# Three of eight pairs of k-tiles of the FFN input products as seven block products instead of eight, in a transformer block on one core

## The reference, cut to what matters

```python
def swiglu(x, w_in, w_out):                  # x 256x2048, w_in 2048x11264, w_out 5632x2048
    gate, up = jnp.split(x @ w_in, 2, axis=-1)
    return (jax.nn.silu(gate) * up) @ w_out
h = x + 0.5 * swiglu(rmsnorm(x, g1), w_in1, w_out1)
...
h = h + 0.5 * swiglu(rmsnorm(h, g2), w_in2, w_out2)
out = rmsnorm(h, g_final)
```

## Time and profile before

| | |
|---|---|
| median of 3 runs | 2148.08 us (2147.76 to 2148.32) |
| span of the profiled execution, first to last instruction | 2145.7 us |
| PE busy | 2137.6 us, 100% |
| DVE busy | 1192.2 us, 56% |
| ACT busy | 1010.0 us, 47% |
| DMA queue of SP | 67.2% of 16 engines |
| mean granted clock of TensorE | 0.999 |

### The profile page before, as it was taken

How to read it: one execution, slowest core, us unless ns; L and a number is a source line. 1 busy time by engine, 2 the same in 40 slices (tenths; PEclk the granted TensorE clock), 3 DMA queues, 4 the chain that set the end, 5 groups by cost and what they waited for, 6 DMA issues and landing times.

```text
span 2145.7 us, 26770 instructions
## 1 busy us (share of the span) xinstructions
PE 2137.6 (100%) x9585; PEld 1774.9 (83%) x9585; DVE 1192.2 (56%) x1187; ACT 1010.0 (47%) x1157; POOL 39.0 (2%) x50
## 2 busy tenths in 40 slices
PE   9999999999999999999999999999999999999998
PEld 8888888888888888888888888888888888888887
DVE  6555555555555576566555656665555555554444
ACT  6444444443444465456544555554444444444343
POOL 0000000000000031000000000000000000000000
PEclk9999999999999999999999999999999999999999
DMA  8766677666666677765587766676676666765554
GB/s 317 240 217 213 212 226 220 213 210 194 226 218 212 217 266 240 237 213 185 177 285 239 234 207 186 201 241 216 211 230 214 212 211 225 223 212 191 194 187 157
DMA packets 183139, 468.15 MB, mean 218 GB/s; under 512 B 16928, under 2 KB 67488, under 8 KB 182944
## 3 DMA queue, kind: packets, MB, share of 16 engines
q1 hardware_dynamic: 180912, 459.91, 67.2%
q0 software_dynamic: 1728, 6.82, 0.9%
q10 hardware_dynamic: 432, 0.53, 0.1%
HBM read 439.41 MB, written 27.79 MB: 218 GB/s over the span
## 4 chain that ended last, share of the span: by engine, by line
PE 99%; issue 0%; DMA 0%; DVE 0%; ACT 0%; POOLq 0%; DVEq 0%; POOL 0%
PE acc L1640 32%; PE acc L1642 32%; PE acc L1643 32%; PE acc L1754 1%; PE aux L1937 0%; PE aux L1910 0%; PE aux L1906 0%; PE aux L1933 0%; PE aux L1932 0%; PE aux L1905 0%; PE aux L1847 0%; DMA arrived<-in_first_cols 0%; PE acc L1719 0%; PE acc L1717 0%; PE acc L1715 0%
## 5 line engine op out<-in xcount | busy, mean ns | idle before, releaser
L1052 DVE TENSOR_TENSOR w_lo<-raw,w_hi 128x1024 fp32r<-128x1024 f32 x765 | 935.9, 1227 | 884.1 <-ACT w_hi L629 882.8
L629 ACT ACTIVATE w_hi<-raw 128x1024 fp32r<-128x1024 f32 x765 | 808.1, 1060 | 1043.1 <-PE acc L1643 1014.4
L1640 PE MATMUL acc<-w_hi,a_hi 128*128 128x512 f32 x1384 | 539.0, 389 | 0.0
L1642 PE MATMUL acc<-w_lo,a_hi 128*128 128x512 f32 x1384 | 538.5, 389 | 0.0
L1643 PE MATMUL acc<-w_hi,a_lo 128*128 128x512 f32 x1384 | 538.5, 389 | 0.0
L1640 PE MATMUL acc<-w_hi,b_hi 128*128 128x512 f32 x1216 | 474.5, 390 | 0.0
L1642 PE MATMUL acc<-w_lo,b_hi 128*128 128x512 f32 x1216 | 473.2, 389 | 0.0
L1643 PE MATMUL acc<-w_hi,b_lo 128*128 128x512 f32 x1216 | 473.2, 389 | 0.0
L1640 PEld LDWEIGHTS acc<-w_hi,a_hi 128*128 128x128 f32 x1384 | 259.8, 188 | 54.7 <-issue 0.9
L1643 PEld LDWEIGHTS acc<-w_hi,a_lo 128*128 128x128 f32 x1384 | 259.8, 188 | 54.1
L1642 PEld LDWEIGHTS acc<-w_lo,a_hi 128*128 128x128 f32 x1384 | 259.8, 188 | 53.5
(11 more groups left out here) (195 smaller groups left out, 687.6 us busy)
## 6 DMA issues: line engine op xcount, KB each, us to landing
raw<-in_ffn_w_in SPq DMA_DIRECT2D x349, 512.0 KB, 4.2
raw<-in_ffn_w_out SPq DMA_DIRECT2D x176, 512.0 KB, 4.2
raw<-in_w_mix_in SPq DMA_DIRECT2D x80, 512.0 KB, 4.6
raw<-in_w_ckv SPq DMA_DIRECT2D x64, 512.0 KB, 4.4
memq<-bounce SPq DMA_DIRECT2D x196, 128.0 KB, 3.8
bounce<-stage SPq DMA_DIRECT2D x37, 512.0 KB, 5.0
raw<-in_w_mix_out SPq DMA_DIRECT2D x32, 512.0 KB, 4.7
raw<-in_w_cq SPq DMA_DIRECT2D x32, 512.0 KB, 4.3
```

The costliest lines, as they stand in the source:

```text
L629: eng.activation(w_hi[:, u % RING], raw[:, u % RING], ACT.Copy).then_inc(w_hi_done, 1)
L1052: eng.tensor_tensor(w_lo[:, u % RING], raw[:, u % RING], w_hi[:, u % RING].bitcast(f32), ALU.subtract).then_inc(w_lo_done, 1)
L1640: eng.matmul(dst, x_hi[:, rows], w_hi[:, slot, i], start=start and i == 0, stop=False)
L1642: eng.matmul(dst, x_hi[:, rows], w_lo[:, slot, i], start=False, stop=False)
```

## The change

In the ten looped passes of each FFN input stage, k-tiles 2s and 2s+1 for s = 0, 1, 2 are handled for gate and up together, as a 2x2 block product: activations in four blocks (2 token halves x 2 k-tiles), weights in four blocks b11, b12 (first k-tile, gate and up columns), b21, b22 (second k-tile). Strassen's scheme gives the four result blocks from seven block products instead of eight. The other five units of gate and five of up stay as they are.

- A pass still has 16 units through the ring (`PAIR_ORDER`): fast 0 (two units), gate 3, gate 4, fast 1 (two units), gate 5, gate 6, fast 2 (two units), gate 7, up 3, up 4 to up 7. The units at places 0, 4 and 8 hold b12 and b11, those at 1, 5 and 9 hold b21 and b22.
- Per fast pair DVE makes three sums of weight blocks in four additions of 512 columns (`weight_sums`, which begins when both units have been loaded; one addition is done in place in `raw`), ACT makes their hi part (1536 columns, `t_hi_part`) and DVE their lo part (`t_lo_part`). The fast units themselves are split as before.
- The sums of activation blocks (`mix_hi`, `mix_lo`) are made once per stage, in the first pair of chunks (`mix_parts`, at places 9, 11, 13).
- PE does 21 matmuls for the two units of a fast pair. Four of the seven sums collect in `tp` and `aux`, which the stage did not use or used for `turn`; `turn` now writes to `stage`.
- At the end of a pass the results are put together: ACT copies one sum, DVE does four additions of 512 columns and two subtractions of 1024 (the second, `up_drained`, in the next pass). PE starts the next pass after `gate_read`, and does the first product into the up banks after `up_read`.
- SP sends `stage` ahead of the load at place 7 and fetches it ahead of the load at place 8.
- The new tiles lie over `h` and `row_gain`, so `h` is loaded again in `ffn_out`, ahead of the loads at its places 4 to 7, and POOL's loads of `row_gain` come after the last fast pair.
- The weights are laid out in the new order on the host, before the kernel.

```diff
+FAST = 3
+def pair_order():
+    plain = [(0, u) for u in range(FAST, U8)] + [(1, u) for u in range(FAST, U8)]
+    order = []
+    for s in range(FAST):
+        order += [("fast", s), ("fast", s)] + plain[:2]
+        plain = plain[2:]
+    return order + plain
...
+GATE_END = PAIR_ORDER.index((0, U8 - 1)) + 1
+UP_START = PAIR_ORDER.index((1, FAST))
+SEND_AT = 7
...
+        sum_p1 = tp[:].rearrange("p (b a) n -> p b (a n)", b=2)[:, 0]
+        sum_p5 = tp[:].rearrange("p (b a) n -> p b (a n)", b=2)[:, 1]
+        sum_p6, sum_p7 = aux[:, 0], aux[:, 1]
+        stage4 = stage[:].rearrange("p t (a n) -> p (t a) n", a=2)
+        copy_p1 = junk
...
+                    for p in range(PAIR):
+                        if p == SEND_AT:
+                            send(number(TURNS, hid) - 1 + j, stage[:], hid_done, silus[base] + j)
+                        if p == SEND_AT + 1:
+                            fetch(number(TURNS, hid) - 1 + j, first=base == FFN1_IN)
+                        load(w, PAIR * j + p, base + PAIR * j, p)
...
+                    if u == RING:
+                        eng.wait_ge(w_used, fast_done(in_base))
+                    if RING <= u < RING + DC:
+                        h_again(in_base, u - RING)
...
+                def fast_hi(j, s):
+                    p = FAST_AT[s]
+                    eng.wait_ge(t1_done, fast_count(base, j, s) + 1)
+                    split(base, j, p, PAIR)
+                    eng.wait_ge(t_summed, fast_count(base, j, s) + 1)
+                    if s:
+                        eng.wait_ge(t_used, fast_count(base, j, s))
+                    eng.activation(t_hi_part[:], t_raw[:], ACT.Copy).then_inc(t_hi_done, 1)
+                    split(base, j, p + 1, PAIR)
+                def pair(j, hid_dst):
+                    for s in range(FAST):
+                        fast_hi(j, s)
+                        split(base, j, FAST_AT[s] + 2, PAIR)
+                        if s == FAST - 1:
+                            fill_hi(turned, number(TURNS, hid) + j, hid_dst, src=stage4)
+                        split(base, j, FAST_AT[s] + 3, PAIR)
+                    for p in range(4 * FAST, PAIR - 3):
+                        split(base, j, p, PAIR)
+                    eng.wait_ge(w_used, base + PAIR * j + FAST_END)
+                    eng.activation(copy_p1, sum_p1, ACT.Copy).then_inc(p1_copied, 1)
+                    split(base, j, PAIR - 3, PAIR)
+                    split(base, j, PAIR - 2, PAIR)
+                    eng.wait_ge(gate_added, fast_pairs[base] + j)
+                    for t in range(NT):
+                        last = eng.activation(stage[:, t], stage[:, t], ACT.Silu,
+                                              scale=rstd[:, stat(rs), t:t + 1])
+                    last.then_inc(silu_done, 1)
+                    split(base, j, PAIR - 1, PAIR)
...
+                def up_drained(j):
+                    eng.wait_ge(gate_read, silus[base] + 1 + j)
+                    eng.wait_ge(w_used, base + PAIR + PAIR * j)
+                    eng.tensor_tensor(shared[:], acc[:, NT:2 * NT], shared[:], ALU.subtract).then_inc(up_read, 1)
...
+                def weight_sums(j, s):
+                    p = FAST_AT[s]
+                    r = p % RING
+                    count = fast_count(base, j, s) + 1
+                    b12, b11, b21, b22 = raw[:, r, 0], raw[:, r, 1], raw[:, r + 1, 0], raw[:, r + 1, 1]
+                    eng.wait_ge(w_loaded[r], loads_of(base, j, p))
+                    eng.wait_ge(w_loaded[r + 1], loads_of(base, j, p + 1))
+                    eng.tensor_tensor(t_raw[:, 0], b12, b22, ALU.add)
+                    eng.tensor_tensor(b12, b12, b11, ALU.add).then_inc(t1_done, 1)
+                    eng.wait_ge(t1_done, count)
+                    eng.tensor_tensor(t_raw[:, 1], b12, b22, ALU.add).then_inc(t2_done, 1)
+                    eng.wait_ge(t2_done, count)
+                    eng.tensor_tensor(t_raw[:, 2], t_raw[:, 1], b21, ALU.add).then_inc(t_summed, 1)
+                def unit_lo(j, p):
+                    split(p, base + PAIR * j + p)
+                def fast_lo(j, s):
+                    weight_sums(j, s)
+                    unit_lo(j, FAST_AT[s])
+                    eng.wait_ge(t_hi_done, fast_count(base, j, s) + 1)
+                    eng.tensor_tensor(t_lo_part[:], t_raw[:], t_hi_part[:].bitcast(f32), ALU.subtract
+                                      ).then_inc(t_lo_done, 1)
+                    unit_lo(j, FAST_AT[s] + 1)
+                def pair(j, hi, lo):
+                    done = fast_pairs[base] + j
+                    for s in range(FAST):
+                        fast_lo(j, s)
+                        if s == FAST - 1:
+                            turn(number(TURNS, hid) - 1 + j, stage4)
+                        unit_lo(j, FAST_AT[s] + 2)
+                        if s == 0:
+                            up_drained(j - 1)
+                        if s == FAST - 1:
+                            fill_lo(split_number(hid) - 1 + j, lo, hi, src=stage4)
+                        unit_lo(j, FAST_AT[s] + 3)
+                        if s == 0:
                             hidden(j - 1)
+                    for p in range(4 * FAST, PAIR - 3):
+                        unit_lo(j, p)
+                    eng.wait_ge(p1_copied, done)
+                    eng.tensor_tensor(shared[:, 0], sum_p6, copy_p1, ALU.add).then_inc(p6_added, 1)
+                    unit_lo(j, PAIR - 3)
+                    eng.wait_ge(p6_added, done)
+                    eng.tensor_tensor(shared[:, 1], shared[:, 0], sum_p7, ALU.subtract).then_inc(p7_added, 1)
+                    eng.wait_ge(w_used, base + PAIR * j + GATE_END)
+                    eng.tensor_tensor(stage[:, 0], acc[:, 0], copy_p1, ALU.add)
+                    eng.wait_ge(p7_added, done)
+                    eng.tensor_tensor(stage[:, 1], acc[:, 1], shared[:, 1], ALU.add).then_inc(gate_added, 1)
+                    unit_lo(j, PAIR - 2)
+                    eng.wait_ge(gate_added, done)
+                    p5 = sum_p5.rearrange("p (a n) -> p a n", a=1).broadcast_to([P, NT, CH])
+                    eng.tensor_tensor(shared[:], shared[:], p5, ALU.subtract).then_inc(gate_read, 1)
+                    unit_lo(j, PAIR - 1)
...
+                def three(dst, x, w, start, stop):
+                    eng.matmul(dst, x[0], w[0], start=start, stop=False)
+                    eng.matmul(dst, x[0], w[1], start=False, stop=False)
+                    return eng.matmul(dst, x[1], w[0], start=False, stop=stop)
+                def block_of(k, t):
+                    rows = slice(t * P, (t + 1) * P)
+                    return hi[:, k, rows], lo[:, k, rows]
+                def ring_block(p, i):
+                    return w_hi[:, p % RING, i], w_lo[:, p % RING, i]
+                def sum_block(i):
+                    return t_hi_part[:, i], t_lo_part[:, i]
+                def fast(j, s):
+                    p = FAST_AT[s]
+                    unit = base + PAIR * j + p
+                    start, stop = s == 0, s == FAST - 1
+                    s3, s1, s2 = [(mix_hi[s][:, i], mix_lo[s][:, i]) for i in range(3)]
+                    eng.wait_ge(w_lo_done, unit + 1)
+                    three(sum_p1, block_of(UK * s, 0), ring_block(p, 1), start, stop)
+                    three(sum_p5, s1, ring_block(p, 0), start, stop).then_inc(w_used, 1)
+                    eng.wait_ge(t_lo_done, fast_count(base, j, s) + 1)
+                    three(sum_p7, s3, sum_block(0), start, stop)
+                    three(sum_p6, s2, sum_block(1), start, stop)
+                    three(acc[:, 1], block_of(UK * s + 1, 1), sum_block(2), start, False).then_inc(t_used, 1)
+                    eng.wait_ge(w_lo_done, unit + 2)
+                    three(acc[:, 0], block_of(UK * s + 1, 0), ring_block(p + 1, 0), start, False)
+                    if s == 0:
+                        eng.wait_ge(up_read, silus[base] + j)
+                    three(acc[:, NT], block_of(UK * s, 1), ring_block(p + 1, 1), start, False).then_inc(w_used, 1)
+                def plain(j, p):
+                    side, u = PAIR_ORDER[p]
+                    eng.wait_ge(w_lo_done, base + PAIR * j + p + 1)
+                    for i in range(UK):
+                        for t in range(NT):
+                            start = p == UP_START and i == 0 and t == 1
+                            stop = u == U8 - 1 and i == UK - 1
+                            last = three(acc[:, NT * side + t], block_of(UK * u + i, t), ring_block(p, i), start, stop)
```

More of the change, by code:

```diff
@@ L26 @@
 OUT_SCALE = float(D) ** -0.5
+PAIR = 2 * U8
+FAST = 3
[6 more added lines that the diff above has]
+    return order + plain
+PAIR_ORDER = pair_order()
+FAST_AT = [PAIR_ORDER.index(("fast", s)) for s in range(FAST)]
+FAST_END = FAST_AT[-1] + 2
+GATE_END = PAIR_ORDER.index((0, U8 - 1)) + 1
+UP_START = PAIR_ORDER.index((1, FAST))
+SEND_AT = 7
+MIX_AT = [9, 11, 13][:FAST]
 FFN1_IN = 0
@@ L346, in encoder_block @@
```

(40 more changed lines are left out.)

160 lines of the change are left out of this document (98 added, 62 removed).

## The result

The changed kernel takes 2176.5 us (2174.8 to 2178.5) against 2148.2 us of the kernel before: 1.0132 times as long, with an interval of 1.0117 to 1.0146. It is slower, as forecast, by 28 us where 42 were predicted.

What follows compares the result with a forecast made beforehand. VectorE was to bound the changed kernel: 39.3 + 1.5 + 0.2 + 4.3 + 0.3 = 45.6 us a pass against 43.52, +42 us over twenty passes, span 2188, time 2190 us. Range 2130 to 2220; the forecast alone 2153 to 2220.

Steps and rivals of the forecast that it cites:

- DVE is the bound of a pass: Looped FFN passes: VectorE's work of 39.3 us plus waits makes 45.6 us, longer than TensorE's 41.49.
- The overlap of 0.09 us: VectorE's queue: an instruction that awaits nothing starts 0.09 us before the one ahead of it ends.
- read as no overlap: Rival for VectorE's new sequences: no overlap, +3.1 us a pass, 2253 us; chance 0.07 together with a fallen clock.
- 0.5 us for ACT's hi part: Each fast pair: VectorE waits 0.5 us for ScalarE's hi part of the weight sums, three times a pass, 1.5 us.
- no wait for the load of place 5: Sums of the second fast pair: 0.3 us of wait at a landing of 4.7, 0 at 4.2, 1.9 at 6.3.
- the wait for the load of place 9: Before the third fast pair's sums: VectorE waits 4.3 us a pass, between 2.2 and 5.2.
- both paths issue it at the same time, right behind a fetch: Load of place 9: slot freed by split 5 and SP's queue behind the fetch coincide; landing taken as 6.3 us.
- The lower bound of 4.2 us: Landing of the load of place 9 in the best case, 4.2 us, giving a wait of 2.2 us.
- `mix_parts` costs nothing: First pair of chunks: some 3 us of VectorE three times, covered by 1.49 us idle per unit; otherwise 9 us a stage.
- PE stays the bound: Rival for the passes: VectorE's waits vanish and TensorE sets their length, 2107 us; to 2143 us, chance 0.20.
- Loads as when alone: Rival for the load waits: landing after 4.2 us, a pass of 43.2 us, 2142 to 2152 us; chance 0.11.
- PE's clock falls: Rival: a TensorE pause of 2 to 3 us each pass lowers its clock, 2238 us; chance 0.07 together with no overlap.

Runs made afterwards that it cites:

- Both doublings: The changed kernel with one VectorE split done twice in each pass: at place 13, 2198.0 us; in another run at place 7, 2173.9 us.
- the fetch at 10: The changed kernel with the fetch ahead of the load of place 10 instead of 8: 2160.1 us.
- the late `mix`: The changed kernel with ScalarE's and VectorE's parts of the activation sums made later in the first pair of chunks: 2167.6 us; also combined with other edits.
- `turn` late: The changed kernel with weight sums' lo part one unit later, activation sums later, fetch at place 12, transpose behind the split of place 11: 2119.7 us.
- the order alone: The changed kernel with both fast units split before ScalarE's hi part and VectorE's lo part of the weight sums: 2137.0 us.
- order, fetch at 12: The changed kernel with both fast units split before the sums' hi and lo parts, and the fetch ahead of the load of place 12: 2142.6 us.
- order, fetch at 10: The changed kernel with both fast units split before the sums' hi and lo parts, and the fetch ahead of the load of place 10: 2141.7 us.

## Why the prediction was right and where it was off

**Right: DVE is the bound of a pass, and the load of place 9 its longest wait.** Both doublings and the fetch show it. The durations held: the lo part of 1536 columns lasts 1.76 us (1.68 + 0.09 was taken), ACT's hi part 1.48. The additions start 0.61, 0.72 and 0.73 us apart (0.59, 0.715, 0.715). The overlap of 0.09 us held in the new sequences too, all of it on this timeline of DVE in one pass of the changed kernel:

```profile
246.93 1.76 DVE L1322 TENSOR_TENSOR t_lo_part<-t_raw,t_hi_part 128x1536 fp32r<-128x1536 f32 x1 [0.42 <-ACT t_hi_part L822]
248.61 3.49 DVE L1185 TENSOR_TENSOR w_lo<-raw,w_hi 128x1024 fp32r<-128x1024 f32 x3
254.97 0.69 DVE L1306 TENSOR_TENSOR t_raw<-raw 128x512 f32<-128x512 f32 x1 [2.88 <-DMA raw<-in_ffn_w_in]
255.58 0.68 DVE L1307 TENSOR_TENSOR raw<-raw 128x512 f32<-128x512 f32 x1
256.30 0.69 DVE L1309 TENSOR_TENSOR t_raw<-raw 128x512 f32<-128x512 f32 x1
257.03 0.69 DVE L1311 TENSOR_TENSOR t_raw<-t_raw,raw 128x512 f32<-128x512 f32 x1
```

246.93 + 1.76 is 0.08 us after the next split started. By the rule of the Trainium skill (VectorE: DVE Perf Modes, Terms), read as no overlap, the sum would have been 2253; the trace disagrees.

**Right: 0.5 us for ACT's hi part** (0.42 measured, three times), and no wait for the load of place 5.

**Mis-sized: the wait for the load of place 9**, 2.64 us against 4.3, and with it nearly the whole error of a pass (44.2 against 45.6). The step that failed is "both paths issue it at the same time, right behind a fetch", with a landing of 6.3 us. DVE's path to the end of split 5 was right, the other was too long. SP's queue in that pass, start and time to the end of issue, then the load's landing and the send's:

```profile
242.89 0.41 SPq L455 DMA_DIRECT2D bounce<-stage  x1
...
245.98 1.97 SPq L464 DMA_DIRECT2D memq<-bounce  x4
248.16 11.20 SPq L448 DMA_DIRECT2D raw<-in_ffn_w_in  x5
...
L448 SPq DMA_DIRECT2D raw<-in_ffn_w_in x1: 352/352/352, 250.0 to 250.0; - x1
...
DMA to landing us min/median/max: 4.9/4.9/4.9
...
L455 SPq DMA_DIRECT2D bounce<-stage x1: 406/406/406, 242.9 to 242.9; - x1
...
DMA to landing us min/median/max: 3.1/3.1/3.1
```

The send landed after 3.1 us, not 4.2, so the fetch was out by 247.9, two us before the load of place 9 at 250.0. That load had only the load of place 8 close ahead, by 1.8 us; the fetch's pieces, with 2.3 to 2.5 us each, had landed. It took 4.9 us, and 4.3 to 5.0 in five passes. A send of on-chip data to a buffer had been priced like a load of weights, and the 6.3 us of three loads 1.1 us apart was too high a price for these neighbours. That is 1.4 us a pass, 28 us in all. The lower bound of 4.2 us was none either: with the fetch at 10 this load lands after 3.8. In the other direction, 0.27 us of a wait for ACT's hi part of what `turn` made was not listed.

**Wrong: `mix_parts` costs nothing, "under the 1.49 us that DVE idles in each unit".** The idle time was there, but it was itself the time in which DVE waits for ACT. The sums that ACT waits for can't be made in it: they stand in DVE's queue behind a split that needs ACT. So cover was read in one engine where the chain goes through two. The prediction named a price of 9 us a stage if the cover were gone. The whole loss outside the loops is 12.0 us for both stages, and the late `mix` takes 6 to 7 of it away. The remaining 5 us, and the longer first passes, were not told apart. The timeline shows at FFN1's entry ACT's table load of 1.28 us behind a wait of 1.35 on `a_lo`, then DVE's 1.30 on silu before its first sums, and PE's 2.56 before the first matmul of the loop; no run took these away.

**The rivals.** *PE stays the bound* did not hold in this order, but it names what another order reaches. *Loads as when alone* gave 2142 to 2152; the landing of 4.9 us lies between 4.2 and 6.3, and passes of 44.2 alone would be 2148 + 14 = 2162, still 10 us above it. *PE's clock falls* once a pass, as the rule of HAM oscillation (the Trainium skill, TensorE: Matmul & The Clock Gate) would have it: in passes it didn't, through the pauses of PE in each (columns of the earlier trace rows):

```profile
212.00:214.00 2.00, 1.92 (x9) 1.27 (x7) 1.97 (x3) 1.73 (x2) 0.00 (x0) 1.00 0.26 107
214.00:216.00 2.00, 1.51 (x6) 1.05 (x6) 1.58 (x2) 2.00 (x3) 0.00 (x0) 1.00 0.21 35
```

This doesn't refute the rival as it stands. It supposed one pause of 2 to 3 us a pass. On PE's timeline of this pass no matmul starts more than 0.7 us late, and the longest idle time in any pass is 1.4 us. Where PE did pause for longer, at the entries, the clock fell (the last section).

So the total came out near the forecast partly by luck, by two errors that offset each other: some 25 us too many in the loops (20 x 45.6 = 912 against 887.3), 12 too few outside them.

## What to carry to other kernels

A scheme that trades matmuls for additions on another engine is decided by the order in that engine's queue. The busy sum was 39.7 us of 41.5 and fitted; what decided were two hand-overs between engines and the distance in time from the instruction that frees a slot to the one that needs its next load. Idle time of an engine is cover for new work only if what it waits for doesn't wait for that new work. And a DMA moved out of a queue's way can cost again where it then runs: beside loads that the same edits have brought close together, or ahead of a reader that now waits for it.

## What the runs showed of the hardware

**PE's clock at the entries.** In the passes of the changed kernel PE pauses, for up to 1.4 us, and stays at 2.4 GHz; at the entries of its loops it doesn't. In the fastest kernel (`turn` late) PE waits 3.94 us for the first lo part of FFN1's loop, as the timeline of PE shows:

```profile
54.82 0.79 PE L1889 MATMUL tp<-w_hi,a_hi 128*128 128x512 f32 x1 [3.94 <-DVE w_lo L1185]
55.41 0.63 PE L1890 MATMUL tp<-w_lo,a_hi 128*128 128x512 f32 x1
55.84 0.63 PE L1891 MATMUL tp<-w_hi,a_lo 128*128 128x512 f32 x1
```

The granted clock of the same kernel around it, in stretches of 2 us, is then 0.50, the level of 1.2 GHz, and matmuls start 0.43 us apart instead of 0.227:

```profile
52.00:54.00 2.00, 0.00 (x0) 0.00 (x0) 1.93 (x4) 1.61 (x2) 0.00 (x0) 0.80 0.00 0
54.00:56.00 2.00, 1.18 (x3) 0.99 (x4) 2.00 (x3) 2.00 (x3) 0.00 (x0) 0.50 0.18 27
...
58.00:60.00 2.00, 2.00 (x6) 1.52 (x6) 2.00 (x3) 0.00 (x0) 0.00 (x0) 0.50 0.70 252
60.00:62.00 2.00, 2.00 (x10) 1.65 (x9) 2.00 (x3) 0.00 (x0) 0.00 (x0) 1.00 0.86 229
```

The twelve matmuls from 54.82 to 60.20 take 5.4 us, where 12 x 0.2267 is 2.7. So the pause of 3.9 us costs up to 6.6. The changed kernel shows the same at the entry of FFN1's loop, after a pause of 2.56 us, and at that of FFN2's, after 1.86 us (0.50 from 1486 to 1488). At FFN1's:

```profile
60.00:62.00 2.00, 1.93 (x5) 1.35 (x5) 2.00 (x3) 1.37 (x2) 0.00 (x0) 0.50 0.51 197
```

The length of the pause alone doesn't decide. In the changed kernel PE also waits 2.50 us before 42.95, in the first pair of chunks, and the granted clock stays at 1.00. With the order alone, where the same code makes the same pause of 2.49 us before 42.34, it falls to 0.50. All four pauses of 3.9 us in the kernels with the late `mix` and three pairs were followed by a fall, pauses of 1.0 to 1.5 us (between 20 and 2100 us of the spans) by none. Nothing here shows what decides in between. One such fall more or less, some 1 to 3 us, can be part of why executions of one kernel differ; no trace of a second execution shows it.

**Loads beside a fetch and beside each other.** The landing of one load of 512 KB, that of place 9, read in five passes of each kernel:

| kernel | load of place 8, ahead by | fetch | landing, us |
|---|---|---|---|
| fetch at 10 | 3.3 to 3.4 us | goes out 0.5 to 0.6 us behind | 3.7 to 4.0 |
| order, fetch at 12 | 1.1 to 1.2 us | over 4 us behind | 4.5 to 4.9 |
| the same, `mix` and `turn` late | 1.1 to 1.2 us | over 4 us behind | 4.1 to 4.8 |
| changed | 1.5 to 2.0 us | its last piece went out 2.1 to 2.6 us ahead | 4.3 to 5.0 |
| order | 0.5 to 0.7 us | its last piece went out 1.0 to 1.2 us ahead | 4.4 to 5.4 |
| order, fetch at 10 | 1.1 to 1.2 us | goes out 0.5 to 0.6 us behind | 5.0 to 5.9 |

A fetch right behind the load doesn't make it late by itself: the first row has the shortest landings. With another load 1.1 to 1.2 us ahead the landing is 4.1 to 4.9 us, and with the fetch as well 5.0 to 5.9. The kernel before showed 4.2 as the median.
